# The first and the last norm of a two-layer decoder step: row squares, a diagonal, transposed rows

## The reference

```
def _rms_norm(x, g):
    y = x * rsqrt(mean(x * x, axis=-1) + EPS)
    return y * g

def _swiglu(h, w_in, w_out):
    gu = h @ w_in
    return (silu(gu[..., :D_FF]) * gu[..., D_FF:]) @ w_out

x = x + 0.5 * _swiglu(_rms_norm(x, ffn1_norm), ...)      # the first thing done
...
x = x + (p[i] @ ple_w_in) * sigmoid(_rms_norm(x, ple_norm) @ ple_w_gate)
y = _rms_norm(x, final_norm)                             # the last thing done
```

## Time and profile before

| | us |
|---|---|
| median of three runs | 2985.13 (2983.31 to 2985.68) |
| the profiled execution | 2977.72 |
| its span, first to last instruction | 2975.9 |
| busy in it: PE, DVE, ACT, POOL | 2836.4, 1376.2, 929.3, 275.7 |
| mean granted TensorE clock | 0.978 of full |

### The profile page before, as it was taken

The page is one execution under the profiler, slowest core; times in us unless marked ns, Lnnn a source line. Parts: engine busy times, 40 slices in busy tenths (PEclk is TensorE's granted clock), DMA queues, the critical chain, the costliest instruction groups (busy, mean ns, idle before and its releaser), DMA issues.

```text
span 2975.9 us, 50054 instructions
## 1 busy us (share of the span) xinstructions
PE 2836.4 (95%) x20858; PEld 2720.3 (91%) x20858; DVE 1376.2 (46%) x1713; ACT 929.3 (31%) x1319; POOL 275.7 (9%) x298
## 2 busy tenths in 40 slices
PE   7999999997999799999999999999989999999997
PEld 6999999995888599999999999999967789999996
DVE  4434347745545454343454443434546544343455
ACT  3222134434333232221332332212346532222233
POOL 4000002301333310000010000000100010000011
PEclk9999999998999799999999999999989999999998
DMA  4222223220011232222222422222302223232221
GB/s 116 85 71 85 85 71 94 77 63 19 17 31 38 66 85 85 85 85 74 71 91 72 132 85 85 85 77 72 106 15 86 96 89 85 85 85 82 73 85 46
DMA packets 306835, 225.60 MB, mean 76 GB/s; under 512 B 8014, under 2 KB 300287, under 8 KB 306687
## 3 DMA queue, kind: packets, MB, share of 16 engines
q1 hardware_dynamic: 306674, 224.30, 25.0%
q0 software_dynamic: 64, 0.00, 0.0%
HBM read 212.14 MB, written 12.13 MB: 75 GB/s over the span
## 4 chain that ended last, share of the span: by engine, by line
PE 88%; DVE 6%; ACT 2%; POOL 2%; issue 1%; DMA 1%; SPq 0%; POOLq 0%; DVEq 0%; ACTq 0%
PE ps L465 76%; PE ps L1438 2%; PE ps L1387 1%; PE ps L1902 1%; DVE ls L1727 1%; PE ps L1909 1%; POOL dx L689 1%; DVE ls_lo L1734 1%; PE ps L1943 0%; DVE w_lo L428 0%; PE ps L1298 0%; DVE ls L1720 0%; DVE xt L1066 0%; PE ps L481 0%; PE ps L1184 0%
## 5 line engine op out<-in xcount | busy, mean ns | idle before, releaser
L465 PE MATMUL ps<-hx_hi,w_hi 128*128 128x320 f32 (+1 forms) x3986 | 859.9, 297 | 13.1 <-DVE hx_lo L2017 8.5
L465 PE MATMUL ps<-hx_lo,w_hi 128*128 128x320 f32 (+1 forms) x3986 | 860.3, 296 | 0.0
L465 PE MATMUL ps<-hx_hi,w_lo 128*128 128x320 f32 (+1 forms) x3986 | 845.8, 293 | 0.0
L418 ACT ACTIVATE w_hi<-raw 128x1024 fp32r<-128x1024 f32 (+2 forms) x378 | 381.9, 1012 | 1302.3 <-PE ps L465 1285.1
L465 PEld LDWEIGHTS ps<-hx_hi,w_hi 128*128 128x128 f32 x3986 | 606.6, 188 | 15.8 <-issue 7.0
L465 PEld LDWEIGHTS ps<-hx_lo,w_hi 128*128 128x128 f32 x3986 | 616.5, 190 | 0.0
L465 PEld LDWEIGHTS ps<-hx_hi,w_lo 128*128 128x128 f32 x3986 | 610.5, 188 | 0.0
L428 DVE TENSOR_TENSOR w_lo<-raw,w_hi 128x1024 fp32r<-128x1024 f32 (+2 forms) x378 | 469.7, 1243 | 130.2 <-ACT w_hi L418 130.0
L465 PE MATMUL ps<-hid_hi,w_hi 128*128 128x320 f32 (+1 forms) x1664 | 358.2, 297 | 12.9 <-DVE of L1162 8.3
L465 PE MATMUL ps<-hid_lo,w_hi 128*128 128x320 f32 (+1 forms) x1664 | 357.4, 296 | 0.0
L465 PE MATMUL ps<-hid_hi,w_lo 128*128 128x320 f32 (+1 forms) x1664 | 356.0, 295 | 0.0
(11 more groups left out here) (373 smaller groups left out, 2447.0 us busy)
## 6 DMA issues: line engine op xcount, KB each, us to landing
raw<-in_ffn_w_in SPq DMA_DIRECT2D x176, 512.0 KB, 4.9
raw<-in_ffn_w_out SPq DMA_DIRECT2D x64, 512.0 KB, 4.0
raw<-in_a_w_in SPq DMA_DIRECT2D x33, 512.0 KB, 4.4
raw<-in_ffn_w_out SPq DMA_DIRECT2D x32, 384.0 KB, 3.5
raw<-in_ple_w_gate SPq DMA_DIRECT2D x16, 512.0 KB, 4.1
raw<-in_w_kv SPq DMA_DIRECT2D x16, 512.0 KB, 3.9
k_page<-in_cache_k SPq DMA_DIRECT2D x16, 512.0 KB, 4.7
v_page<-in_cache_v SPq DMA_DIRECT2D x16, 512.0 KB, 4.4
```

Source lines behind the costliest of these rows:

```text
L418: nc.scalar.activation(w_hi[:, m, 0:k], s.view(m, slot), ACT.Copy).then_inc(w_hi_done, 1)
L465: last = nc.tensor.matmul(TILE[m][:, c0:c1], w[:, m, k], h[:, k, c0:c1], start=k == 0 and a == 0, stop=k == k_all - 1 and a == 2)
```

## The change

The first norm no longer uses `ssum`. ScalarE squares the rows of x as they were loaded (rows on partitions) and sums each row in the same instruction (`accum_out`), five row tiles; the root and the reciprocal are taken on one column for each row tile; VectorE multiplies the identity by that column, and TensorE multiplies ones by these diagonals, which puts the factor of each row on all partitions. VectorE copies it to `rs`. TensorE does this ahead of the fifth k of the second tile of the first unit. The copies of x tiles 1, 3 and 5 out of PSUM are made by ScalarE. The gain loads are issued by ScalarE. Each x load has its own semaphore. TensorE takes the sample rows first and the gains after the first tile.

The last norm: in the last product stage ScalarE also writes x times the final gain into `yT` for each tile. TensorE transposes the left four tiles of it while the stage still runs, and tiles 4 and 5 too; ScalarE and VectorE copy the left halves to `y_rows`. After the last tile come the remaining transposes, then five products of `ssum` (128 rows each) with one column of ones, so that the sums lie on the rows' partitions; root and reciprocal on five columns; and the rows are multiplied by them, from PSUM and from `y_rows`, and stored from five row buffers. The first turn of Pool's loop over the sums is written out.

```
@@ setup: loads @@
-            for name, row in (("ffn1_norm", FFN1), ("mix_norm", MIX), ("ffn2_norm", FFN2), ("ple_norm", PLE)):
-                sp.dma_start(gain_rows[row:row + 2 * KD], A[name].rearrange("l (k c) -> (l k) c", c=P)).then_inc(gain_in, 16)
...
+            for name, row in (("ffn1_norm", FFN1), ("mix_norm", MIX), ("ffn2_norm", FFN2), ("ple_norm", PLE)):
+                act.dma_start(gain_rows[row:row + 2 * KD], A[name].rearrange("l (k c) -> (l k) c", c=P)).then_inc(gain_in, 16)
...
@@ multiply @@
             if isinstance(u, int) and n + u == 0:
-                pe.wait_ge(setup_ev, 2 + 2 * m)
+                pe.wait_ge(setup_ev, (3, EARLY_FILLS)[m])
...
-                if s.stats and isinstance(u, int) and u == m == 0 and k == (k_all // 2 if n else k_all - 1):
+                if n + m == 1 and isinstance(u, int) and u == 0 and k == k_all // 2:
+                    x_scale_rows(pe)
+                if s.stats and n and isinstance(u, int) and u == m == 0 and k == k_all // 2:
                     pe_stats(pe, s, s.n["stat"])
...
+        def x_scale_rows(pe):
+            pe.wait_ge(const_done, 1)
+            pe.wait_ge(x_diag_done, NT)
+            pe.wait_ge(setup_ev, EARLY_FILLS)
+            pe.wait_ge(x_by_scalar, 3)
+            for c0, c1 in ((0, P), (P, 2 * P), (2 * P, HC), (HC, 3 * P), (3 * P, 4 * P), (4 * P, T)):
+                i, n = c0 // P, x_rows_of(c0 // P)
+                last = nc.tensor.matmul(STAT[:, c0 // HC, c0 % HC:c0 % HC + c1 - c0], ones[0:n],
+                                        x_diag[0:n, i, c0 - i * P:c1 - i * P], start=True, stop=True)
+            last.then_inc(stat_done, 1)
...
@@ the end: TensorE @@
+        def pe_left(pe, i):
+            n = y_size(i)
+            pe.wait_ge(y_done, KD // 2)
+            if i == PT:
+                pe.wait_ge(y_left_ev[0], 1)
+            for q in range(KD // 2):
+                last = nc.tensor.transpose(ps[0:n, left_bank(i), q * P:(q + 1) * P], yT[:, q, i * P:i * P + n], ident[:])
+            last.then_inc(y_left_tr, 1)
+        def pe_end(pe, s):
+            multiply(pe, s, 0, 0)
+            multiply(pe, s, 0, 1)
+            multiply(pe, s, 1, 0)
+            multiply(pe, s, 1, 1)
+            multiply(pe, s, 2, 0)
...
+            for i in range(PT):
+                pe_left(pe, i)
+            multiply(pe, s, 2, 1)
+            pe_left(pe, PT)
+            multiply(pe, s, 3, 0)
+            pe.wait_ge(y_left_ev[0], 3)
+            pe.wait_ge(y_left_ev[1], 2)
+            for k in range(KD // 2, KD // 2 + 2):
+                for i in range(PT):
+                    pe_right(pe, i, k)
+            multiply(pe, s, 3, 1)
+            pe.wait_ge(evac[0], s.n["unit"] + s.units)
+            for k in range(KD // 2, KD // 2 + 2):
+                pe_right(pe, PT, k)
+            for k in range(KD // 2 + 2, KD):
+                for i in range(NT):
+                    last = pe_right(pe, i, k)
+            last.then_inc(y_right_tr, 1)
+            pe.wait_ge(ssum_done, KD * (s.n["sum"] + 1))
+            for i in range(NT):
+                n = y_size(i)
+                last = nc.tensor.matmul(ps[0:n, 1, i:i + 1], ssum[:, i * P:i * P + n], ones[:, 0:1], start=True, stop=True)
+            last.then_inc(stat_done, 1)
...
@@ Pool @@
-                if s.kind == "setup":
-                    for j in range(KD):
-                        pool_renorm(pool, s, j, j % 2)
...
@@ ScalarE @@
+                            if s.end:
+                                j = u * 2 + m
+                                nc.scalar.activation(yT[:, j], xT[:, j], ACT.Copy, scale=gain[:, FIN + j:FIN + j + 1]).then_inc(y_done, 1)
...
+                    for i in range(3):
+                        row_square(i)
+                    x_high(0, setup_ev, 3)
+                    x_fill(1)
+                    x_high(1, x_by_scalar, 1)
                     split_hi(act, (products[0], 0, 0), 0)
+                    x_fill(3)
+                    x_high(2, setup_ev, 4)
+                    x_high(3, x_by_scalar, 2)
+                    x_fill(5)
+                    x_high(4, setup_ev, 5)
+                    x_high(5, x_by_scalar, 3)
+                    row_square(3)
+                    x_high(6, setup_ev, 6)
+                    x_high(7, setup_ev, 7)
                     split_hi(act, (products[0], 0, 0), 1)
+                    row_square(PT)
...
@@ VectorE, final @@
-                    dve_stats(dve, s.n["stat"])
...
+                    dve.wait_ge(col_std, 1)
+                    nc.vector.reciprocal(rs_col[:, 0:PT], std_col[:, 0:PT]).then_inc(col_rs, 1)
...
+                    for i in (0, 2, PT):
+                        y_scale(dve, i)
```

More of the change, by code:

```diff
@@ L315, in ffn, with ple @@
                         after=after if last else None, sums=last)
[L317 removed]
+        def ple(layer, after, end=False):
             product("pin", KD // 2, PK, PK, pair_loads(A["ple_w_in"][layer], 0, 0, PK), PR)
[L319 removed]
+            product("ple", KD // 2, KD, KD, pair_loads(A["ple_w_gate"][layer], 0), HX, stats=True, after=after, sums=True,
+                    end=end)
         def rows_of(src, dst):
@@ L329, in rows_of @@
             return out
-        stage("setup", after=FFN1, sums=True)
+        stage("setup", after=FFN1)
         ffn("ffn1", 0, MIX, between=("late", "p"))
@@ L351, in program @@
         ffn("ffn2", 1, PLE + KD)
-        ple(1, None)
-        stage("final", fills=rows_of(yT, None))
+        ple(1, None, end=True)
+        stage("final")
         count = dict.fromkeys(("unit", "eb", "gu", "hid", "hx", "sum", "stat", "ple", "p", "gs", "tok", "rows"), 0)
@@ L361, in program @@
             count["tok"] += len(s.fills)
-            count["stat"] += s.stats or s.kind == "final"
+            count["stat"] += s.stats
             count["sum"] += s.sums
@@ new lines, in y_scale @@
+        def y_scale(eng, i):
+            n, par = y_size(i), i % 2
+            for at_, src in ((HALF_D, ps[0:n, y_bank(i)]), (0, y_rows[0:n, i, 0:HALF_D])):
+                to, by = y_rows[0:n, i, at_:at_ + HALF_D], rs_col[0:n, i:i + 1]
+                if par:
+                    nc.scalar.activation(to, src, ACT.Copy, scale=by).then_inc(y_scaled[1], 1)
+                else:
+                    nc.vector.tensor_scalar(to, src, by, None, ALU.mult).then_inc(y_scaled[0], 1)
+        def pe_left(pe, i):
[6 more added lines that the diff above has]
+            last.then_inc(y_left_tr, 1)
@@ L2193, in _ @@
                     pool_zero(pool, s)
-                if s.kind == "setup":
-                    for j in range(KD):
-                        pool_renorm(pool, s, j, j % 2)
-                elif s.kind in ("upd", "ple") and s.sums:
-                    with pool.Fori(0, s.units) as u:
+                if s.kind in ("upd", "ple") and s.sums:
+                    for m in range(2):
+                        pool_renorm(pool, s, m, m)
+                    with pool.Fori(1, s.units) as u:
                         for m in range(2):
@@ L2277, in body @@
                         for m in range(2):
+                            if s.end and (u, m) == (2, 1):
+                                y_left(act, 1)
+                                y_left(act, 3)
                             split_hi(act, split, m)
```

214 lines of the change are left out of this document (158 added, 56 removed).

## The result

The changed kernel took 2961.95 us (median of four, 2959.15 to 2962.85) against 2984.22 (2977.34 to 2985.68) for the kernel before beside it: ratio 0.9933, 95% interval 0.9919 to 0.9948. By the medians that is 22.3 us faster, by the ratio 20.0 (15.5 to 24.2), where 20.8 were forecast; 2964.3 was forecast for the median. Its profiled execution took 2962.85, with a span of 2961.1.

What follows compares the result with a forecast made beforehand. TensorE, busy 95% of the span, was taken as the bound, so only its waits at start and end could pay. Start 11.7 plus end 9.1 gave 20.8 us, from a median of 2985.13 to 2964.3; range 2957 to 2973.

Steps and rivals of the forecast that it cites:

- Loads: Start: last x rows land at 11.3 (9.5 to 13), sharing the transfer with earlier weights; TensorE starts at 11.4.
- Transposes: Start: TensorE's transposes of x and gains run from 11.4 to 19.9, a full one taking 0.22.
- Tile 0 and 1: First two product tiles: 19.95 to 26.3, then 26.5 to 35.1; second read (start mark) at 35.6, gain 11.7.
- Inserted transposes: Last product stage: transposes put between TensorE's products cost 3.6 us on the path, 7.6 at half rate.
- Tail: After the last product: 17.9 us instead of 30.6 (bounds 15.8 to 20), ended by transfers; end gain 9.1.
- Sum: Whole kernel: 11.7 + 9.1 = 20.8 us gained; profiled execution to 2956.9, median to 2964.3.
- clock remark: Start: array begins at 1.2 GHz, reaches 2.4 by 20.3, falls after idle 1.99 us; new products at full rate.
- 1 (start bound by something else): Start: x rows landing at 13 or row sums of 1.75 give back 3 to 4 us; 2968; chance 0.17.
- 2: First products stay at 1.2 GHz, 1.6 us late, tail's small products 0.6; gain 18.6, 2966.5; chance 0.13.
- 3: End pays nothing: inserted transposes 4.0 us more, stores 2.1 more; total gain 14.7, 2970.4; chance 0.10.
- 4: Last product stage: ScalarE's y copy delays weights, TensorE waits in eight tiles; 2989 if it takes 5 us; chance 0.02.
- 5: Start: the new order waits on itself, a ScalarE copy held behind a landing; gain under 6; chance 0.05.

Runs made afterwards that it cites:

- start_only: Only the start half of the change (setup and first unit) applied to the kernel before: median 2968.50 us, ratio 0.9958.
- tail_transposes: Changed kernel with all transposes of the final rows moved behind the last product, sums' columns in another bank: median 2956.85 us, ratio 0.9917.
- changed_again: The changed kernel, unedited, run once more on another chip: median 2961.09 us, ratio 0.9931 to the kernel before.
- before_again: The kernel before, unedited, run again for a second profile: median 2985.36 us, ratio 0.9998.
- end_only: Only the end half of the change (last product stage and final norm) applied to the kernel before: median 2969.09 us, ratio 0.9960.
- decay_transposes_thrice: Changed kernel with the ten small decay-row transposes at the head of the gated-delta stage issued three times: median 2964.02 us, ratio 0.9936.
- tail_and_copies: Changed kernel with all final transposes behind the last product and copies of x tiles 1, 3, 5 back on VectorE: median 2956.04 us, ratio 0.9916.

## Why the prediction was right

By its own steps:

- **Loads.** x down at 11.3, TensorE from 11.4: 10.9 and 11.04. The chain of waits of after begins with them: 8.21 of issue to landing for x_sample, where 7.4 were read in before. Over the six profiles in which nothing between x and the mark was edited, or only the queue of the gains, x landed from 10.7 to 12.4.
- **Transposes.** 41 from 11.4 to 19.9 were forecast, and they took from 11.04 to 18.16. The step was mis-sized by 1.4: 28 full ones took 5.06, a mean of 0.18, instead of the 0.22 I split out of a mixed row. The 0.22 was right for the first ones (0.213 from one start to the next); the last ones went at 0.109, since the clock rose at 16.85. The mark hardly gained by it. The chain of waits of after runs from 15.05 to 23.11 through VectorE's copies and low parts, and in start_only, where the clock rose at 14.26 and the transposes were done at 16.8, TensorE then waited 1.40 for the weights' low parts.
- **Tile 0 and 1.** 19.95 to 26.5 forecast, 18.44 to 25.75 measured; the low parts did come close, one by 0.27 too late. Diagonals forecast for 28.6, done at 28.3, asked for at 29.03. The row sum costs 0.18 on top of its 1.06 (1.06 to 1.75 were the bounds), a diagonal 0.21 (0 to 0.68), the twelve exact matmuls 1.6 in place of 2.2. From the first transpose to the mark 23.04, where 24.2 was forecast, and 23.0 to 23.1 in all six of those profiles. Start gain 13.2 for 11.7 in this pair.
- **Inserted transposes.** 3.6 forecast, 3.05 measured, no gap ahead of them. By tail_transposes the whole of it was avoidable, which the prediction did not see: it priced the insertion rightly and never asked what TensorE does in the 3.77 us for which it stands idle in the tail.
- **Tail.** 17.9 forecast, 17.5 measured: last x tile 3.05 (3.1), y copy 4.4 (4.5), transposes done 5.3 (5.6), small products 7.5 (8.4), first row tile ready 9.4 (10.2), last 11.5 (12.4), transfers at about 400 GB/s until past 2959. The stores end it, as said. End gain 13.1 - 3.05 = 10.0 for 9.1 in this pair.
- **Sum.** 23.2 for 20.8. With both profiles in the long form of the stage, 2984.1 - 2961.1 = 23.0; the medians give 22.3, and 19.2 on the chip of changed_again.

One pair of profiles says too much. The mark lies from 45.8 to 47.3 in the three profiles with the old start (mean 46.4: before, before_again, end_only) and from 33.9 to 35.5 in the five with the new one (mean 34.8: after, changed_again, start_only, tail_transposes, decay_transposes_thrice): the start is worth 11.7, as forecast. In the same way the part behind the stage takes 1969.6 to 1970.8 in four profiles with the old end (mean 1970.3) and 1959.0 to 1963.0 in seven with the new one (mean 1960.9): 9.4, where 9.1 was forecast. That sums to 21.1 for 20.8. Some of this closeness is luck: the forecast set the new mark at 35.6, 0.8 over that mean, and took the old one from a profile which was itself 0.8 over its mean.

Two sentences of the prediction were wrong without harm to its number. It said that the profiled execution lies 7.4 below the median by something the edits don't touch and would keep that distance. The first fits the stage, whose long and short forms differ by 8; the second failed: the profile of after fell on the long form, so that the 2956.9 forecast for it was missed by 6 us, while the median was met within 2.4. That is in part luck too, as a median of few executions depends on how many of them had the long form. It also said that TensorE runs without a pause behind the start mark. It does not: in the gated-delta stage of before it is busy for 289.9 of 327.0 us, and that is where executions of one kernel differ.

The clock remark was right, though the view seems to say otherwise. Windows of before print the granted clock as 1.00 over the slow first transposes:

```profile
12.00:14.00 2.00, 2.00 (x13) 1.88 (x14) 0.00 (x0) 0.00 (x0) 1.55 (x7) 1.00 1.20 294
16.00:18.00 2.00, 2.00 (x11) 1.88 (x9) 2.00 (x5) 0.01 (x1) 1.65 (x6) 1.00 1.12 215
22.00:24.00 2.00, 2.00 (x11) 2.00 (x10) 1.80 (x3) 1.35 (x2) 1.86 (x2) 0.50 0.00 1
```

```profile
16.72 1.43 PE L2687 MATMUL ps<-ident,x_rows 128*128 128x128 f32 x11
```

So the array started at the 1.2 GHz level and was at 2.4 GHz before its first product, in before as in after. The fall of before came after the idle 1.99 us, and its first products ran at 0.50.

Of the rivals: 1 (start bound by something else) did not come, x landed at 10.9 in after and at 12.4 at the latest, and a row sum cost 0.18. 2 did not come at the start: in after the first products ran at full rate (0.43 a pair) right behind 7 us of transposes. Its other half did: the small products of the tail ran at 0.50. At 2.17 they still took less than the 2.7 in the sum, where 0.27 each had been taken. The Trainium skill ("TensorE: Matmul & The Clock Gate", Part 4: PE-mode transpose) says that transposes do not count as work for the clock. The traces of this case disagree with it at both ends. At the start the clock rose 3.5 to 6.6 us after TensorE's first transpose, in all 13 traces before its first product, when it had done nothing but transposes. In the tail, the clock fell 5.3 to 5.7 us behind the last product in the seven profiles with the end of after, where TensorE idles from 2944.3 (after) for 3.77. In tail_transposes and tail_and_copies, where transposes fill that time, it fell 8.4 and 8.7 us behind it. By the rule both kinds should look alike. These transposes are made by `nc.tensor.transpose`; their records in the trace do not name a mode of the engine. 3 did not come: 3.05 and 17.5. 4 did not come: the copy took 0.76. 5 did not come.

## What to carry to other kernels

Price inserted work against the idle time of the tail as well as against the stream: transposes put between products cost their whole length, the same ones behind the last product cost nothing and kept the clock up for the small products behind them. To move a wait, look at what stands behind it on the other engines; sums moved alone gave 3.44 us of the wait back through VectorE. Before an edit is credited or blamed, cut both spans at marks around stages that it does not touch: here such a stage differed by 8 us, more than a third of the gain. Compare more than one profile of each side: the start gain was 13.2 in one pair and 11.7 over eight profiles. And where a view prints a full clock, see whether the trace has a record for it; the pace of like instructions tells the same.

## What was not expected of the hardware

- The gated-delta stage has TensorE busy for 289.9 to 297.8 of 327 to 335 us, with many short waits, and its granted clock falls to 0.50 several times at a different list of moments from one execution to the next. In before_again the list is 17.1 us from 705, 6.8 from 742, 6.8 from 821, 3.4 from 865 and 6.8 from 991; in after it is the same list some 12.3 us sooner; in the first profile of before it is 20.5 from 700 and nothing until 987. tail_and_copies (331.0) and decay_transposes_thrice (332.2) have lists in between.
- What chooses between the lists was not found. The moment of arrival does not (678.2 and 678.3 gave one each in one kernel, 666.7 gave either in two).
- TensorE's clock was at half rate when the program began and rose while TensorE did transposes alone: they followed each other every 0.213 us before that moment and every 0.109 after it, in all 13 traces.
- An activation with a row sum issues a second instruction of 0.18 to 0.19 us.
- VectorE scales 512 columns by a column in 0.47 to 0.48 from SBUF and in 0.73 to 0.75 from PSUM; ScalarE takes 0.68 to 0.72 for either.
